# Last expert pair of a mixture-of-experts layer: other PSUM banks, later weight rows, a scatter in two halves, and one weight load issued earlier

## The chip, the cores and the metric

One Trainium2 chip, one of its cores. The metric is the device time of one execution in microseconds (us). The kernel before takes 551.63 us (median of 3 runs, 550.75 to 552.73). Engines: PE (TensorE), DVE (VectorE), ACT (ScalarE), POOL (GpSimd), and SP, which issues most of the DMAs.

## The reference

A decoder layer on 512 tokens of width 1024, float32: attention and a short convolution with their projections, a residual and a LayerNorm, then a mixture of 32 experts (each token goes to 2 of them), a residual and a second LayerNorm. The part that matters here:

```python
h2 = (x * (1.0 + scale2) + shift2).reshape(bsz * seq, d)
moe = _hierarchical_moe(h2, ...)   # per expert: silu(h @ w_gate) * (h @ w_up), weighted, @ w_down
x = _layer_norm(DEEPNORM_ALPHA * x + gate2 * moe, ln2_g[l], ln2_b[l])
```

An expert has w_gate and w_up of 1024 x 256 and w_down of 256 x 1024: three blocks of 1 MB each, 96 MB over all experts.

## The kernel before

The first 240 us compute the attention, the convolution and the modulation vectors; until about 300 us come the output projection, the first LayerNorm (x1) and the router. Every expert has 64 slots for tokens. Experts are worked on in 16 pairs (`pair(j)`, numbers 2j and 2j+1); the rows of a pair are 128 partitions, 64 for each expert.

For a pair, POOL **gathers** the rows of h2 from DRAM by an indirect DMA (L621), PE transposes them (`expert_rows`, L1612) and ACT copies them out (L833). For each expert PE then runs gate and up together (`gates`, `gate_up`, L1622, 32 instructions), ACT the silu (L846), DVE the product (`hidden`, L1247), PE a transpose of it (`turn`, L1640), ACT a copy (`hid_t`, L840), PE the down projection (`finish`, `down`, L1631) into a PSUM bank that `down_bank` names, and DVE scales its result out of that bank into the buffer ysb (`y_out`, L1256, two instructions). When both experts of a pair are out, POOL **scatters** ysb to y_dram, 2 rows for each token, by an indirect DMA (`scatter`, L627). `y_out` counts in the semaphore y_ev, and `finish(n)` waits until the bank it writes has been read: y_ev >= n if the down projection before it used the same bank.

Weights come through SP's DMA queue in a written order: `load_gu(n)` (gate and up, ring of 8 buffers, L460) and `load_dn(n)` (ring of 6, L471). A load waits for the expert that last used its buffer. The first loads wait for what else lies in their buffers: the up half of expert 7 for the last tiles of x1 (`x1_last`, which DVE writes at L1178), w_dn of expert 5 for the stores of h2 (`st_h2`, issued by ACT at L790), and the gate half of expert 8 for `gates(0)`.

The last pair, 15, is not scattered. PE builds rows of weights (`weight_rows`, L1660) from the diagonals `diag`, DVE makes from them a matrix hot_w (`last_hot`, L1280 to L1287), and PE multiplies it with ysb of that pair straight into the sum of each token tile (`last_rows`, L1737). The rest of a tile is x1 and the two rows of y_dram: SP loads x1 of tiles 0 and 1 (L532) and, when all scatters are down, eight blocks y_tok of 512 KB (L537). The residual x1 of tiles 2 and 3 was held in PSUM (tile 2 in banks 0 and 1, tile 3 in banks 4 and 5) and ACT copies it out (L892). DVE adds seven terms to x1 (`first_terms`, L1346), PE adds x1 to the sum (`other_terms`, L1744), and statistics, scaling and stores of the four tiles follow. Tiles are taken in the order 1, 2, 3, 0.

The order around the change is that of the code: each engine runs its list in order and waits on semaphores.

## Time and profile before

| | us |
|---|---|
| median of 3 runs | 551.63 |
| the profiled execution's own time | 551.87 |
| its span | 550.1 |
| PE busy | 509.8 |
| DVE busy | 285.4 |
| ACT busy | 105.5 |
| POOL busy | 101.6 |

The span is what the traced instructions cover; the execution's own time is 1.8 us longer. Busy time is the sum over the whole span. DMA traffic is given in GB/s, and as the mean busy share of the core's 16 DMA engines.

### The profile page before, as it was taken

What the parts mean: (1) busy time and instruction counts of PE and PEld (TensorE: products, weight loads), DVE (VectorE), ACT (ScalarE), POOL (GpSimd) and SP (SyncE); (2) the same over time, 40 slices, a digit from 0 to 9 for tenths busy, and PEclk for the clock granted to TensorE, in tenths of its full rate; (3) what the DMA queues carried; (4) which work ended last, traced back from release to release, by engine and by line L of the source; (5) the groups of instructions that cost most, each with busy time, mean ns of one, the idle gap of its engine ahead of it and who ended that gap; (6) DMA issues with size and microseconds to landing.
All of it is one profiled execution on the core that took longest, in us unless ns stands there. A gap on an engine that the chain in (4) does not pass through costs nothing.

```text
span 550.1 us, 6473 instructions
## 1 busy us (share of the span) xinstructions
PE 509.8 (93%) x2516; PEld 274.5 (50%) x2516; DVE 285.4 (52%) x520; ACT 105.5 (19%) x173; POOL 101.6 (18%) x111
## 2 busy tenths in 40 slices
PE   3999999999999999999996999999998799898983
PEld 2445468744444444444583555555554355444531
DVE  4664999763937393263889732232222122213388
ACT  1000211233223231200232311111111111121030
POOL 2000000061306040030452111111211011210015
PEclk9999999999999999999997999999999899989998
DMA  8999679954640244269998999999999999999763
GB/s 254 358 361 352 207 237 309 309 212 153 227 155 1 77 146 174 75 245 418 413 391 310 388 405 420 414 416 417 414 417 416 416 415 416 416 416 418 312 251 153
DMA packets 71280, 169.22 MB, mean 308 GB/s; under 512 B 7902, under 2 KB 45842, under 8 KB 63056
## 3 DMA queue, kind: packets, MB, share of 16 engines
q1 hardware_dynamic: 64304, 152.22, 73.2%
q10 hardware_dynamic: 2480, 8.44, 4.0%
q0 software_dynamic: 4464, 8.12, 3.9%
q8 instruction: 21, 0.34, 0.2%
q14 instruction: 11, 0.09, 0.0%
HBM read 159.60 MB, written 17.30 MB: 322 GB/s over the span
## 4 chain that ended last, share of the span: by engine, by line
PE 61%; DVE 14%; DMA 11%; SPq 9%; issue 3%; ACT 1%; POOL 0%; DVEq 0%; POOLq 0%; ACTq 0%
PE ps L1622 17%; PE ps L1492 11%; PE ps L1538 10%; PE ps L1631 9%; DVE acc_rows L935 5%; SPq L414 4%; DMA w_gu<-in_w_up_dram 4%; PE ps L1612 3%; PE ps L1462 3%; DMA ada_stage<-in_w_ada_dram 3%; DMA w_stage<-in_w_in_dram 2%; PE ps L1481 2%; DMA y_tok<-y_dram 2%; PE ps L1526 2%; DMA y_dram<-ysb,slot_row 1%
## 5 line engine op out<-in xcount | busy, mean ns | idle before, releaser
L1622 PE MATMUL ps<-w_gu,xT 128*64 128x256 f32 x1024 | 119.3, 386 | 3.4 <-issue 1.6
L1622 PEld LDWEIGHTS ps<-w_gu,xT 128*64 128x64 f32 x1024 | 72.0, 138 | 40.5 <-issue 3.4
L1492 PE MATMUL ps<-hT,w_stage 128*128 128x512 f32 x192 | 84.8, 595 | 0.0
L1256 DVE TENSOR_TENSOR ysb<-ps,rows_gate 64x512 f32<-64x512 f32 x64 | 44.1, 689 | 61.8 <-PE ps L1631 61.3
L1631 PE MATMUL ps<-w_dn,hidT 128*64 128x512 f32 x256 | 62.9, 612 | 7.8 <-issue 6.1
L935 DVE SCALAR_TENSOR_TENSOR acc_rows<-ada_stage,csil,acc_rows 128x256 f32<-128x256 f32 x112 | 55.2, 493 | 4.0
L1247 DVE TENSOR_TENSOR hid<-ps,silu_sb 128x128 f32<-128x128 f32 x32 | 9.3, 292 | 91.9 <-ACT silu_sb L846 91.9
L1492 PEld LDWEIGHTS ps<-hT,w_stage 128*128 128x128 f32 x192 | 35.5, 190 | 41.0 <-issue 41.0
L1538 PE MATMUL ps<-wo,mixT 128*128 128x512 f32 (+1 forms) x144 | 55.6, 545 | 0.0
L1403 PE MATMUL ps<-hT,w_first 128*128 128x512 f32 x96 | 45.5, 621 | 0.9 <-DVE hT L961 0.9
L627 POOL DMA_INDIRECT y_dram<-ysb,slot_row x15 | 15.1, 1009 | 151.8 <-DVE ysb L1256 151.8
L1538 PEld LDWEIGHTS ps<-wo,mixT 128*128 128x128 f32 x144 | 27.2, 190 | 27.1 <-issue 26.3
L1631 PEld LDWEIGHTS ps<-w_dn,hidT 128*64 128x64 f32 x256 | 17.3, 138 | 31.3 <-issue 25.9
L846 ACT ACTIVATE silu_sb<-ps 128x128 f32<-128x128 f32 x32 | 8.9, 277 | 115.9 <-PE ps L1622 115.9
L1462 PE MATMUL ps<-w_stage,hT 128*128 128x256 f32 x128 | 28.1, 380 | 0.2 <-DMA w_stage<-in_w_in_dram 0.2
L1403 PEld LDWEIGHTS ps<-hT,w_first 128*128 128x128 f32 x96 | 18.2, 199 | 20.1 <-issue 20.1
L1462 PEld LDWEIGHTS ps<-w_stage,hT 128*128 128x128 f32 x128 | 24.2, 190 | 4.3 <-DMA w_stage<-in_w_in_dram 0.6
L983 DVE TENSOR_TENSOR_SCAN stay<-stay,block_end 128x1280 f32<-128x1280 f32 x8 | 24.1, 3015 | 3.4 <-POOL stay L586 3.4
L583 POOL TENSOR_SCALAR_AFFINE_SELECT stay<-stay 128x384 f32<-128x384 f32 x8 | 5.3, 658 | 101.0 <-ACT stay L727 101.0
L947 DVE SCALAR_TENSOR_TENSOR acc_cols<-ada_in,csil,acc_cols 128x512 f32<-128x512 f32 (+1 forms) x35 | 22.6, 645 | 2.3 <-DMA ada_in<-in_w_ada_dram 1.1
L621 POOL DMA_INDIRECT xg<-h_dram,slot_tok x16 | 16.9, 1054 | 37.0 <-PE ps L1622 23.3
L1612 PEld LDWEIGHTS ps<-ident,xg 128*128 128x128 f32 x128 | 15.5, 194 | 6.6 <-issue 5.8
(213 smaller groups left out, 499.2 us busy)
## 6 DMA issues: line engine op xcount, KB each, us to landing
w_gu<-in_w_gate_dram SPq DMA_DIRECT2D x32, 1024.0 KB, 20.3
w_gu<-in_w_up_dram SPq DMA_DIRECT2D x32, 1024.0 KB, 23.3
w_dn<-in_w_down_dram SPq DMA_DIRECT2D x32, 1024.0 KB, 24.3
ada_stage<-in_w_ada_dram SPq DMA_DIRECT2D x16, 1024.0 KB, 7.8
w_stage<-in_w_in_dram SPq DMA_DIRECT2D x9, 1024.0 KB, 10.1
ada_in<-in_w_ada_dram SPq DMA_DIRECT2D x12, 512.0 KB, 9.5
y_dram<-zeros ACTq DMA_DIRECT2D x4, 1024.0 KB, 5.8
wo<-in_w_out_dram SPq DMA_DIRECT2D x2, 2048.0 KB, 13.3
```

The source lines that it names most:

```text
L414: sp.dma_start(ada_in[c][:, ks, s], rows[:, ks, s * D + k * P:s * D + (k + m) * P]).then_inc(ld_ada[c][half], 16)
L935: link(w.scalar_tensor_tensor(out=acc, in0=st[:, k], scalar=csil[:, 3, k:k + 1], in1=acc, op0=ALU.mult, op1=ALU.add))
L947: ins = w.scalar_tensor_tensor(out=acc, in0=ada_in[c][:, k], scalar=csil[:, 3, k:k + 1], in1=acc, op0=ALU.mult, op1=ALU.add)
L983: w.tensor_tensor_scan(out=st[:, 0:ZW][:, ::-1], data0=st[:, 0:ZW][:, ::-1], data1=block_end[:, ::-1], initial=1.0, op0=ALU.mult, op1=ALU. ...
L1256: ins = w.tensor_tensor(to[e * HD:(e + 1) * HD, b * 512:(b + 1) * 512], ps[b * HD:(b + 1) * HD, down_bank(y), :], gate2r[b * HD:(b + 1) * ...
L1403: ins = t.matmul(ps[:, n], w_first[:, k, n * P:(n + 1) * P], hT[:, k], start=k == 0, stop=k == KC - 1)
L1462: ins = t.matmul(dst[:, 0:CW], hT[:, k, i * P:(i + 1) * P], st[:, k], start=k == 0, stop=k == KC - 1)
L1492: ins = t.matmul(ps[:, 6], st[:, k, (f % 2) * P:(f % 2 + 1) * P], hT[:, k], start=k == 0, stop=k == KC - 1)
L1538: ins = t.matmul(ps[:, 4 + q % 4, 0:width], mixT[:, i, k], wo[n][:, k, col:col + width], start=k == 0, stop=k == KC - 1)
L1612: ins = t.transpose(flat[:, ROWS_AT + k * P:ROWS_AT + (k + 1) * P], by_channel(xg[rows_buffer(j)])[:, k], ident[:])
L1622: ins = t.matmul(ps[a * SLOTS:(a + 1) * SLOTS, GATE_BANK[e], 0:2 * P], rows_in[:, k, e * SLOTS:(e + 1) * SLOTS], weights[:, :, k, a * P:(a ...
L1631: ins = t.matmul(ps[b * SLOTS:(b + 1) * SLOTS, bank, :], hidT[e][:, a * SLOTS:(a + 1) * SLOTS], weights[:, a, b * 512:(b + 1) * 512], star ...
```

## The change

Five edits:

- **Banks.** `down_bank` gives expert 29 bank 4 and expert 31 bank 5 (before: 29 in bank 7, 31 in bank 2). For that, x1 of tiles 2 and 3 is copied out of PSUM by ACT in pair 14, behind `hid_t(28, 0)`, and no longer at the end; the copies go to a buffer of their own, `x1_sb`, in the place of the weights of expert 28. `finish(29)` waits for the copy of tile 3.
- **Weight rows.** PE builds them behind `gates(30)` and no longer ahead of it, into banks 0 and 1 (before: 3 and 6). DVE makes hot_w behind `hidden(30, 0)` and no longer ahead of it, in one multiply over 1024 columns instead of two over 512.
- **Scatter.** The rows of pair 14 go in two indirect DMAs of 64 partitions, each as soon as its expert is out. The second takes its row numbers from `late_row`, which DVE copies once.
- **Load order.** SP issues w_dn of expert 5, behind the wait for the stores of h2, ahead of the wait for `x1_last` and the up half of expert 7.
- Waits on the scatters are counted anew.

Part of the branch for overflowing experts, in which only counts change, is left out of the diff.

```diff
--- before.py
+++ after.py
@@ -153,12 +153,13 @@
         g1r = at("g1r", [P, D], REST + 48 * KB)
         b1r = at("b1r", [P, D], REST + 52 * KB)
 
-        x1_back = at("x1_back", [P, TC, D], 0)
+        x1_back = at("x1_back", [P, 2, D], 0)
         norm2 = at("norm2", [1, 2, D], 0)
         slot_id = at("slot_id", [P, TC, 2, P], EXP_B + 8 * KB)
         ones_back = at("ones_back", [P, P], EXP_B + 12 * KB)
         hot_w = at("hot_w", [P, TC, 2, P], PAIR2)
         zeros = at("zeros", [P, D], PAIR2)
+        x1_sb = at("x1_sb", [P, 2, D], PAIR2 + 4 * KB)
         y_tok = [at(f"y_tok{i}", [P, 2, D], PAIR1 + (i + 1) * 8 * KB) for i in range(TC)]
         diag = at("diag", [P, TC, 2, P], REST + 48 * KB)
         g2r = at("g2r", [P, D], PAIR1)
@@ -188,6 +189,7 @@
         wk = sm("wk", [P, 2, TC])
         mh = sm("mh", [P, 1])
         last_row = sm("last_row", [P, 1])
+        late_row = sm("late_row", [P, 1], I32)
         tile_total = sm("tile_total", [P, 2])
         colsb = sm("colsb", [P, 2 * KC])
         b_cols = sm("b_cols", [P, 2, KC])
@@ -380,7 +382,11 @@
 
         def down_bank(n):
 
-            return 2 if n == NE - 1 else 7
+            return {NE - 3: 4, NE - 1: 5}.get(n, 7)
+
+        def x1_rows_of(i):
+
+            return x1_back[:, i] if i < 2 else x1_sb[:, i - 2]
 
         def h2T_of(i):
 
@@ -496,11 +502,11 @@
             load_gu_part(GU_RING - 1, 0)
             sp.wait_ge(logit_done, TC)
             load_gu(5)
-            sp.wait_ge(x1_last, 2 + 2 * len(X1_BY_DVE))
-            load_gu_part(GU_RING - 1, 1)
             for n in range(2):
                 sp.wait_ge(st_h2[n], 32)
             load_dn(5)
+            sp.wait_ge(x1_last, 2 + 2 * len(X1_BY_DVE))
+            load_gu_part(GU_RING - 1, 1)
             load_gu(GU_RING)
             dn_next = DN_RING
             for n in range(GU_RING + 1, NE):
@@ -524,14 +530,14 @@
                                          ).then_inc(ov_ld, 16)
                         sp.dma_start(w_dn[e][:], w_down[0, bass.ds(ex, 1)].rearrange("o (a p) n -> p (o a) n", p=P)
                                      ).then_inc(ov_ld, 16)
-                sp.wait_ge(scattered[0], 16 * (NPAIR // Y_RING + NOVP))
+                sp.wait_ge(scattered[0], 16 * (NPAIR // Y_RING + 1 + NOVP))
 
 
             sp.wait_ge(n2_done, 4)
             for i in (1, 0):
                 sp.dma_start(x1_back[:, i], x1_dram.rearrange("(i p) n -> i p n", p=P)[i]).then_inc(ld_x1[i], 16)
             for n in range(Y_RING):
-                sp.wait_ge(scattered[n], 16 * ((NPAIR - n) // Y_RING))
+                sp.wait_ge(scattered[n], 16 * (NPAIR // Y_RING + 1 if n == 0 else NPAIR // Y_RING - 1))
             for i in TAIL:
                 for k in range(2):
                     sp.dma_start(y_tok[i][:, k], y_dram.rearrange("(i p k) n -> i k p n", p=P, k=2)[i, k]
@@ -539,7 +545,7 @@
             out_rows = out[0].rearrange("(i p) n -> i p n", p=P)
             for i in (2, 1, 3):
                 sp.wait_ge(fin_done[i], 1)
-                sp.dma_start(out_rows[i], x1_back[:, i]).then_inc(st_out, 16)
+                sp.dma_start(out_rows[i], x1_rows_of(i)).then_inc(st_out, 16)
             for n in range(2):
                 cols = slice(n * 512, (n + 1) * 512)
                 sp.wait_ge(fin_done[0], n + 1)
@@ -621,6 +627,13 @@
                 g.indirect_dma_start(out=buf[:], out_offset=None, in_=h2_dram,
                                      in_offset=bass.IndirectOffsetOnAxis(ap=slot_tok[:, j:j + 1], axis=0),
                                      bounds_check=T - 1, oob_is_err=False).then_inc(sem_done, 16)
+
+            def scatter_half(j, e, buf, sem_done):
+
+                rows_to = slot_row[0:SLOTS, j:j + 1] if e == 0 else late_row[0:SLOTS, 0:1]
+                g.indirect_dma_start(out=y_dram, out_offset=bass.IndirectOffsetOnAxis(ap=rows_to, axis=0),
+                                     in_=buf[e * SLOTS:(e + 1) * SLOTS], in_offset=None,
+                                     bounds_check=2 * T - 1, oob_is_err=False).then_inc(sem_done, 16)
 
             def scatter(j, buf, sem_done):
 
@@ -666,8 +679,14 @@
                     pool.wait_ge(gu_done, NE - 6)
                     g.iota(slot_id[:], [[2 * P, TC], [1, 2], [2, P]], base=0, channel_multiplier=0,
                            allow_small_or_imprecise_dtypes=True).then_inc(slot_ids, 1)
-                pool.wait_ge(y_ev, 2 * j + 2)
-                scatter(j, ysb[j % Y_RING], scattered[j % Y_RING])
+                if j == NPAIR - 2:
+                    pool.wait_ge(diag_done, 2 * TC + 2)
+                    for e in range(2):
+                        pool.wait_ge(y_ev, 2 * j + 1 + e)
+                        scatter_half(j, e, ysb[j % Y_RING], scattered[j % Y_RING])
+                else:
+                    pool.wait_ge(y_ev, 2 * j + 2)
+                    scatter(j, ysb[j % Y_RING], scattered[j % Y_RING])
 
             pool.wait_ge(flag_ready, 1)
             more = pool.value_load(flag[0:1, 0:1], min_val=0, max_val=NOVB)
@@ -862,6 +881,9 @@
                 if j == NPAIR - 3:
                     norm_rows()
                 hid_t(2 * j, 0)
+                if j == NPAIR - 2:
+                    for i in (2, 3):
+                        s.copy(x1_rows_of(i), x1_held(i)).then_inc(ld_x1[i], 16)
                 silu(2 * j + 1, 1)
                 if j + 1 < NPAIR:
                     xe_copy(j + 1)
@@ -887,9 +909,6 @@
                         act.wait_ge(tr_done, NE + 2 * j + e + 1)
                         s.copy(hidT[e][:], ps[:, GATE_BANK[e], TURN:TURN + P]).then_inc(tr_ev, 1)
 
-
-            for i in (2, 3):
-                s.copy(x1_back[:, i], x1_held(i)).then_inc(ld_x1[i], 16)
 
             act.wait_ge(summed, 2)
             s.activation(x1_back[:, 1], flat[:, 0:D], ACT.Identity, accum_out=tile_total[:, 0:1]).then_inc(totals, 1)
@@ -1261,8 +1280,9 @@
             def pair(j):
                 if j == NPAIR - 1:
                     y_out(2 * j - 1, 1)
+                hidden(2 * j, 0)
+                if j == NPAIR - 1:
                     last_hot()
-                hidden(2 * j, 0)
                 if 0 < j < NPAIR - 1:
                     y_out(2 * j - 1, 1)
                 if j == 0:
@@ -1278,12 +1298,9 @@
                 dve.wait_ge(slot_ids, 1)
                 dve.wait_ge(w_rows, 1)
                 link(w.tensor_copy(last_row[:], slot_row[:, NPAIR - 1:NPAIR]))
-                for b in range(2):
-                    some = slice(b * TC // 2, (b + 1) * TC // 2)
-                    did(w.scalar_tensor_tensor(out=hot_w[:, some].rearrange("p c k t -> p (c k t)"),
-                                               in0=slot_id[:, some].rearrange("p c k t -> p (c k t)"), scalar=last_row[:, 0:1],
-                                               in1=ps[:, (3, GATE_BANK[1])[b]], op0=ALU.is_equal, op1=ALU.mult))
-                settle()
+                link(w.scalar_tensor_tensor(out=hot_w.rearrange("p c k t -> p (c k t)"),
+                                            in0=slot_id.rearrange("p c k t -> p (c k t)"), scalar=last_row[:, 0:1],
+                                            in1=flat[:, 0:2 * T], op0=ALU.is_equal, op1=ALU.mult))
                 w.tensor_tensor(hot_w[:, :, 0], hot_w[:, :, 0], hot_w[:, :, 1], ALU.add).then_inc(hot_ready, 1)
 
             dve.wait_ge(row_ev, 8)
@@ -1296,6 +1313,7 @@
             for i in range(TC):
                 for k in range(2):
                     w.tensor_scalar(diag[:, i, k], ident[:], wk[:, k, i:i + 1], None, ALU.mult).then_inc(diag_done, 1)
+            w.tensor_copy(late_row[0:SLOTS], slot_row[SLOTS:2 * SLOTS, NPAIR - 2:NPAIR - 1]).then_inc(diag_done, 1)
             pair(NPAIR - 2)
             pair(NPAIR - 1)
             y_out(NE - 1, 1)
...
@@ -1324,13 +1342,13 @@
             def centre(i, src):
 
                 settle()
-                w.scalar_tensor_tensor(out=x1_back[:, i], in0=src, scalar=mv[:, TC + i, 0:1], in1=g2r[:],
+                w.scalar_tensor_tensor(out=x1_rows_of(i), in0=src, scalar=mv[:, TC + i, 0:1], in1=g2r[:],
                                        op0=ALU.subtract, op1=ALU.mult).then_inc(centred, 1)
 
             def finish(i, cols):
 
                 dve.wait_ge(rstd_done, norm_at(TC + i) + 1)
-                w.scalar_tensor_tensor(out=x1_back[:, i, cols], in0=x1_back[:, i, cols], scalar=rstd[:, TC + i:TC + i + 1],
+                w.scalar_tensor_tensor(out=x1_rows_of(i)[:, cols], in0=x1_rows_of(i)[:, cols], scalar=rstd[:, TC + i:TC + i + 1],
                                        in1=bb2r[:, cols], op0=ALU.mult, op1=ALU.add).then_inc(fin_done[i], 1)
 
             def tile_sum(i):
@@ -1343,8 +1361,8 @@
                 dve.wait_ge(ld_x1[i], 16)
                 for k in range(n):
                     dve.wait_ge(ld_y[i][k], 16)
-                    ins = w.scalar_tensor_tensor(out=x1_back[:, i], in0=y_tok[i][:, k], scalar=wk[:, k, i:i + 1],
-                                                 in1=x1_back[:, i], op0=ALU.mult, op1=ALU.add)
+                    ins = w.scalar_tensor_tensor(out=x1_rows_of(i), in0=y_tok[i][:, k], scalar=wk[:, k, i:i + 1],
+                                                 in1=x1_rows_of(i), op0=ALU.mult, op1=ALU.add)
                     if k + 1 < n:
                         link(ins)
                 ins.then_inc(partial, 1)
@@ -1650,14 +1668,17 @@
                 pe.wait_ge(ld_dn[n % DN_RING], 16 * (n // DN_RING + 1))
                 if n >= 1:
                     pe.wait_ge(y_ev, n if down_bank(n) == down_bank(n - 1) else n - 1)
+                if n == NE - 3:
+                    pe.wait_ge(ld_x1[3], 16)
                 down(n % 2, w_dn[n % DN_RING], dn_done, down_bank(n))
 
             def weight_rows():
 
                 pe.wait_ge(diag_done, 2 * TC + 1)
+                pe.wait_ge(ld_x1[2], 16)
                 for i in range(TC):
                     for k in range(2):
-                        ins = t.matmul(ps[:, (3, GATE_BANK[1])[i // 2], (2 * (i % 2) + k) * P:(2 * (i % 2) + k + 1) * P], ones_back[:], diag[:, i, k], start=True, stop=True)
+                        ins = t.matmul(flat[:, (2 * i + k) * P:(2 * i + k + 1) * P], ones_back[:], diag[:, i, k], start=True, stop=True)
                 ins.then_inc(w_rows, 1)
 
             def norm_rows():
@@ -1675,9 +1696,10 @@
                     turn(2 * j - 1, 1)
                     if j == NPAIR - 1:
                         finish(2 * j - 1)
-                        weight_rows()
                     pe.wait_ge(xe_ev, j + 1)
                     gates(2 * j)
+                    if j == NPAIR - 1:
+                        weight_rows()
                     if j < NPAIR - 1:
                         finish(2 * j - 1)
                     if j == NPAIR - 3:
@@ -1741,7 +1763,7 @@
 
                 pe.wait_ge(partial, TAIL.index(i) + 1)
                 for n in range(2):
-                    ins = t.matmul(ps[:, sum_bank(i) + n], ident[:], x1_back[:, i, n * 512:(n + 1) * 512],
+                    ins = t.matmul(ps[:, sum_bank(i) + n], ident[:], x1_rows_of(i)[:, n * 512:(n + 1) * 512],
                                    start=False, stop=not by_pe)
                     if not by_pe:
                         ins.then_inc(summed, 1)
@@ -1752,11 +1774,9 @@
                                  start=False, stop=True).then_inc(summed, 1)
 
             pe.wait_ge(y_ev, NE)
-            pe.wait_ge(ld_x1[2], 16)
             last_rows(1)
             last_rows(2)
             other_terms(1, False)
-            pe.wait_ge(ld_x1[3], 16)
             last_rows(3)
             other_terms(2, False)
             last_rows(0)
```

**PE**, the last pair: `down` of expert 28, `turn` and `down` of expert 29, and the weight rows between the down projection and the gate and up of expert 30 (L1660). Before:

```order
L1631 MATMUL ps<-w_dn_61,hidT_164 64x512 x4
L1640 MATMUL ps<-ident,hid_141 128x128
L1631 MATMUL ps<-w_dn_62,hidT_165 64x512 x4
L1660 MATMUL ps<-diag,ones_back 128x128 x8
L1622 MATMUL ps<-w_gu_55,xT_117 64x256 x16
L1640 MATMUL ps<-ident,hid_140 128x128
L1622 MATMUL ps<-w_gu_56,xT_117 64x256 x16
```

The same place in the changed kernel, whose line numbers are its own:

```order
L1649 MATMUL ps<-w_dn_61,hidT_166 64x512 x4
L1658 MATMUL ps<-ident,hid_142 128x128
L1649 MATMUL ps<-w_dn_62,hidT_167 64x512 x4
L1640 MATMUL ps<-w_gu_55,xT_117 64x256 x16
L1681 MATMUL ps<-diag,ones_back 128x128 x8
L1658 MATMUL ps<-ident,hid_141 128x128
L1640 MATMUL ps<-w_gu_56,xT_117 64x256 x16
```

The eight matmuls of the weight rows moved from ahead of the gate and up of expert 30 to behind it; what PE does is otherwise in the same order.

**SP**, the first loads that wait, about 283 to 307 us; w_gu_54 and w_dn_62 belong to expert 5, w_gu_56 to expert 7, w_gu_49 to expert 8, and the waits stand in brackets. Before:

```order
L460 DMA w_gu_54<-in_w_up_dram 128x2048
L460 DMA w_gu_56<-in_w_up_dram 128x2048 [waits x1_last]
L471 DMA w_dn_62<-in_w_down_dram 128x2x1024 [waits st_h21,st_h20]
L460 DMA w_gu_49<-in_w_gate_dram 128x2048 [waits gu_done]
L460 DMA w_gu_49<-in_w_up_dram 128x2048
```

In the changed kernel:

```order
L466 DMA w_gu_54<-in_w_up_dram 128x2048
L477 DMA w_dn_62<-in_w_down_dram 128x2x1024 [waits st_h21,st_h20]
L466 DMA w_gu_56<-in_w_up_dram 128x2048 [waits x1_last]
L466 DMA w_gu_49<-in_w_gate_dram 128x2048 [waits gu_done]
L466 DMA w_gu_49<-in_w_up_dram 128x2048
```

Two rows changed places: w_dn of expert 5 now waits for its own two semaphores alone.

## Rows read from the trace of the kernel before

**Rows 1.** The page, the span in 40 equal slices: DMA share in tenths, and GB/s.

```profile
DMA  8999679954640244269998999999999999999763
GB/s 254 358 361 352 207 237 309 309 212 153 227 155 1 77 146 174 75 245 418 413 391 310 388 405 420 414 416 417 414 417 416 416 415 416 416 416 418 312 251 153
```

**Rows 2.** The chain that ended last: start us, us, what.

```profile
476.45 22.89 DMA w_gu<-in_w_up_dram
...
511.75 6.79 DMA y_dram<-ysb,slot_row
...
519.39 9.22 DMA y_tok<-y_dram
```

**Rows 3.** Timeline 503 to 517 us: start, us, engine line op, operands, [idle before <-releaser].

```profile
503.11 0.28 ACT L846 ACTIVATE silu_sb<-ps 128x128 f32<-128x128 f32 x1 [3.76 <-PE ps L1622]
506.32 0.27 ACT L840 COPY hidT<-ps 128x128 f32<-128x128 f32 x1 [1.12 <-PE ps L1640]
507.60 1.94 PE L1631 MATMUL ps<-w_dn,hidT 128*64 128x512 f32 x8 [1.32 <-DVE ysb L1256]
509.47 2.05 PE L1660 MATMUL ps<-diag,ones_back 128*128 128x128 f32 x16
509.58 1.39 DVE L1256 TENSOR_TENSOR ysb<-ps,rows_gate 64x512 f32<-64x512 f32 x2 [2.12 <-PE ps L1631]
511.45 3.67 PE L1622 MATMUL ps<-w_gu,xT 128*64 128x256 f32 x32
515.83 0.33 PE L1640 MATMUL ps<-ident,hid 128*128 128x128 f32 x1 [0.70 <-DVE hid L1247]
516.09 3.67 PE L1622 MATMUL ps<-w_gu,xT 128*64 128x256 f32 x32
```

**Rows 4.** Loads of w_gu: the up half of expert 31, issued at 490.1 us.

```profile
DMA to landing us min/median/max: 25.4/25.4/25.4
```

**Rows 5.** Loads of x1 for tiles 1 and 0, issued at 500.1 and 501.6 us.

```profile
DMA to landing us min/median/max: 22.0/22.2/22.3
```

**Rows 6.** The eight loads of y_tok, issued from 518.55 to 522.0 us.

```profile
DMA to landing us min/median/max: 6.3/10.4/12.9
```

**Rows 7.** Timeline 522 to 529 us, the end of the last pair.

```profile
522.73 1.93 ACT L892 COPY x_back<-ps 128x1024 f32<-128x1024 f32 x2 [0.69 <-issue]
524.08 1.39 DVE L1256 TENSOR_TENSOR ysb<-ps,rows_gate 64x512 f32<-64x512 f32 x2 [1.16 <-PE ps L1631]
527.13 1.28 DVE L1346 SCALAR_TENSOR_TENSOR x_back<-y_tok,wk,x_back 128x1024 f32<-128x1024 f32 x1 [0.35 <-DMA y_tok<-y_dram]
528.71 6.32 DVE L1346 SCALAR_TENSOR_TENSOR x_back<-y_tok,wk,x_back 128x1024 f32<-128x1024 f32 x5 [0.29 <-DMA y_tok<-y_dram]
```

**Rows 8.** Windows: us, busy (x) of PE, PEld, DVE, ACT, POOL, PEclk, DMA share, GB/s.

```profile
299.00:300.00 1.00, 1.00 (x3) 0.47 (x2) 1.00 (x2) 0.00 (x0) 0.90 (x2) 0.50 0.12 49
301.00:302.00 1.00, 1.00 (x3) 0.19 (x1) 0.93 (x4) 0.00 (x0) 0.78 (x1) 1.00 0.17 54
306.00:309.00 3.00, 2.20 (x19) 1.20 (x17) 1.63 (x10) 0.54 (x2) 0.00 (x0) 1.00 1.03 403
518.00:519.00 1.00, 1.00 (x14) 0.64 (x12) 0.00 (x0) 0.00 (x0) 0.00 (x0) 1.00 0.27 111
```

**Rows 9.** SP's timeline: w_dn of expert 5, gate half of expert 8.

```profile
302.09 0.38 SPq L471 DMA_DIRECT2D w_dn<-in_w_down_dram  x1
307.30 0.33 SPq L460 DMA_DIRECT2D w_gu<-in_w_gate_dram  x1
```

**Rows 10.** Landing of w_gu of expert 8, issued at 307.3 and 307.7 us.

```profile
DMA to landing us min/median/max: 5.6/6.6/7.7
```

**Rows 11.** Landing of gathers 0 and 1, issued at 298.0 and 301.2 us; PE's timeline.

```profile
DMA to landing us min/median/max: 4.1/4.1/4.1
...
DMA to landing us min/median/max: 7.7/7.7/7.7
...
302.15 1.16 PE L1612 MATMUL ps<-ident,xg 128*128 128x128 f32 x8
```

More of the change, by code:

```diff
@@ L1305, in _ @@
                 with dve.Fori(0, NOVP) as j:
-                    dve.wait_ge(scattered[0], 16 * (NPAIR // Y_RING) + 16 * j)
+                    dve.wait_ge(scattered[0], 16 * (NPAIR // Y_RING + 1) + 16 * j)
                     for e in range(2):
```

## The prediction

> **What bounds the kernel now.** I first read the page's 40 slices [rows 1]. From about 310 us to 508 us the core moves 388 to 420 GB/s in nearly every slice, with the share of DMA time at nine tenths or more: the stream of expert weights runs without a gap. Only the last three slices fall off. Then the chain that ended last [rows 2]: at its end stand a weight load (up half of expert 29, issued 476.45, down at 499.34), the last scatter (6.79 us) and the loads of y_tok (9.22 us). So the last 50 us are a race between the DMA queues and PE, and I took the timeline there and asked for each load when it landed.
>
> PE in that stretch [rows 3]: `finish(29)` starts at 507.60, having waited 1.32 us for `y_out(28)` because both use bank 7; weight rows 509.47; `gates(30)` 511.45; a wait of 0.70 for the product; `gates(31)` 516.09. The up half of expert 31 was issued at 490.1 and took 25.4 us [rows 4]: it is down at 515.5, only 0.6 us before PE uses it.
>
> The views that decide are those of landings. The x1 tiles were issued at 500.1 and 501.6 and need 22.3 and 22.0 us [rows 5]: 522.4 and 523.6. The eight y_tok loads, issued from 518.55, land first after 6.3 us (524.85) and last after 12.9 (522.0 + 12.9 = 534.9) [rows 6]. Eight tiles between 523.6 and 534.9 are 1.3 to 1.4 us for each, which is what 512 KB take at 400 GB/s. So the first y_tok comes one tile's time behind the last x1 tile, although it was issued 5 us before that tile was down. In the same time the window 518 to 519 shows a DMA share of 0.27 and 111 GB/s [rows 8]: about 4 of 16 engines still work on what was queued, the others are empty. A load is down when the slowest engine has done its part. The y_tok tiles are therefore held by a few engines that are late, not by their issue.
>
> DVE ends the last pair at 524.08 + 1.39 = 525.5 and goes through seven terms; it waits 0.35 and 0.29 us for y_tok and then runs on without a wait, one term in 1.3 us, as fast as the late engines deliver [rows 7]. What follows (statistics, scaling, stores) hangs on these terms.
>
> **The change part by part.**
>
> *Bank of expert 29.* `finish(29)` then needs only its transposed input, whose copy ends at 506.32 + 0.27 = 506.59 [rows 3]. It starts at about 506.65: 0.95 us earlier. Its new wait, for ACT's copy of tile 3, costs nothing: both copies take 1.93 us [rows 7] and are put into a gap of ACT of 3.76 us that ends at 503.11 [rows 3], so they are done at about 501.3. Behind `finish(29)` on PE is `gates(30)`.
>
> *Weight rows.* Without them ahead of it (509.47 to 511.45, 1.98 us) `gates(30)` could start 0.95 + 1.98 = 2.9 us earlier, at 508.5. Its weights are the question. The trace gives no landing for the up half of expert 30. The bounds are 499.34 (expert 29's, [rows 2]) and 511.45, when PE used it without a wait [rows 3]. Six blocks of 1 MB come down between 499.34 and 515.5, 2.7 us each; two of them behind this one, so 515.5 - 5.4 = 510.1. I take 510.1. Then 3.67 for `gates(30)`, 1.98 for the weight rows, which cover the wait of 0.70, and 0.3 for `turn(30)`: `gates(31)` at 516.05, against 516.09. The 2.9 us won by the two edits are spent on a weight load that is not there yet (1.6) and on the weight rows that now stand between two pieces of work (1.3). Ends: with the weights at 508.5 or before, `gates(31)` is held by its own load at 515.5, a gain of 0.6; with 511.45 it starts at 517.4, a loss of 1.3. `last_hot` on DVE has until 525.5 and costs nothing there (DVE is idle for most of this time); the second half of hot_w in one instruction instead of two changes nothing either.
>
> *Bank of expert 31 and the copies at the end.* ACT's two copies end at 524.66 [rows 7], before `y_out(31)` at 525.5, which PE waits for as well. Taking them away gives nothing.
>
> *Scatter in halves.* `y_out(29)`, at 509.58 [rows 3], comes 0.95 us earlier, and with it the second half: issued at 510.8 instead of 511.75 [rows 2]. The first half is issued some 3 us before. Landing of the second: not later than a whole one, 510.8 + 6.8 = 517.6; not earlier than its packets in a quiet queue, the 4.1 us of the first gather [rows 11], 514.9. I take 516.5, so y_tok is issued 2 us earlier, and the quick engines finish earlier. The late ones have x1 tiles in front until 523.6 whatever the issue time, so the term is 0. Its ends: 0 and, if the issue did count, what DVE can take: its waits (0.64) and what PE gains (0.6), 1.2 us.
>
> The Trainium skill, "DMA: Bandwidth & Descriptors", section "Anatomy of one DMA", fits a DMA issued by POOL as 2.0 us plus its bytes at 436 GB/s. By that a half scatter of 256 KB would need 2.6 us as an estimate, where the whole one shows 6.79 [rows 2]; the sum would stay what it is, since the x1 tiles stand in front all the same.
>
> *w_dn of expert 5 earlier.* It was issued at 302.09 [rows 9]; the new place lets it go when the stores of h2 are down, some 6 us earlier. There the DMA is nearly idle (shares 0.12 and 0.17 [rows 8]), and 1 MB is 2.5 us at 416 GB/s. But the hole is moved, not filled. The next load, expert 8, waits for `gates(0)` and is issued at 307.30 [rows 9]. In the kernel before, w_dn and two gathers keep the engines full until then (306 to 309: share 1.03 [rows 8]), and expert 8 lands at 307.7 + 7.7 = 315.4 [rows 10], so its 2 MB (5.0 us) began at about 310. Afterwards they can begin at 307.3 plus 0.8 us from issue to movement (as y_tok: 518.55 to 519.39), 308.1, plus 0.6 for a gather that still shares the queue: 308.7. Against that, the first gather, which PE takes at once at 302.15 [rows 11], now shares the engines with w_dn. Its delay is between 0 and 3.6 us (a gather behind a load took 7.7 us, this one 4.1 [rows 11]). I take 0.8, because w_dn ends at about 301.5 and the gather's own bytes are 0.6 us. `gates(0)` and the load of expert 8 come 0.8 later: 309.5 instead of 310. From there the stream has no gap [rows 1], so its end moves as its beginning: **0.5 us earlier**, between 1.3 earlier and 2.3 later.
>
> Sum: 0 + 0 + 0 + 0 - 0.5, from the profiled execution's own 551.87, gives 551.4. That execution is 0.24 us above the median of 551.63, so on the scale of the medians 551.1 to 551.4; I say **551.3**. Less than 0.3% (1.65 us, about what a measurement of this kernel can tell from no change).
>
> **The rivals.**
>
> *Faster: issue and PE do count.* If the late engines catch up, or are others in the changed kernel, the tail is held by DVE and by `gates(31)`: 0.6 to its load, 0.64 of waits, and 0.5 to 1.0 of the earlier stream, 1.7 to 2.3 us: 549.7. For it: y_tok moves 2 us earlier, and the chain runs through it [rows 2]. Against it: landings of x1 and y_tok follow each other without a hole [rows 5, 6].
>
> *Slower: the first gather is held up.* If gather 0, with a load queued in front and one beside it, takes the 7.7 us of gather 1 [rows 11], PE starts 3.6 us later and expert 8's load with it: 308.1 + 3.6 = 311.7, and the gather beside it is then through; 1.7 to 2.3 us later than now. The stream ends that much later, and so does everything behind it: 553.8. It decides from a delay of 1.3 us on, where the 0.5 us of gain is gone. Against it: the engines run dry in that stretch, so w_dn can be in the way for its own 2.5 us only.
>
> The same page of the Trainium skill, section "Queues, rings and completion order", says that an engine takes turns between its queues, packet by packet. By that the gather is delayed by about its own length, an estimate nearer to my 0.8 than to 3.6.
>
> *Same time, other reason: weight rows in the way.* If expert 30's weights land at 511.45 only, the tail is up to 1.3 us later, less the 0.5: 552.4, still within the bound unless it comes together with the gather.
>
> **How the numbers follow.** Forecast 0.60, weight rows in the way 0.08 (also "no change"), issue counts 0.21, gather held up 0.08, small ends of both 0.03. So faster by over 0.3%: 0.22; within: 0.67; slower: 0.11. The likeliest is the forecast, 551.3. The range goes down to 549.3, a little below the faster rival, and up to 552.9, which takes in the weight rows but not all of the gather.
>
> **What would show it.** In the changed profile: `down` of expert 29 with no wait for DVE, at about 506.6; a wait of `gates(30)` for DMA of 1 to 2 us; weight rows ahead of `turn(30)`, and `gates(31)` within 0.6 us of 516; y_tok issued near 516.9, but the first of them landing 8 us later instead of 6.3; the DVE terms still waiting for y_tok. Early on: w_dn of expert 5 issued near 296.4, the first gather landing in about 5 us, and a DMA share clearly under 1 between 306 and 308. I am wrong if y_tok lands as much earlier as it is issued, if `gates(30)` finds its weights at 508.5, or if the first gather is late by more than 1.3 us.

## The result, and the profile after

The changed kernel takes 553.36 us (median of 21 runs, 551.59 to 555.68), the kernel before in the same comparison 551.67 (21 runs, 550.00 to 552.73): a ratio of 1.0034, with a 95% interval of 1.0023 to 1.0045. It is slower by 1.7 us (difference of the medians). I had forecast 551.3 and no change, with a range up to 552.9; the slower side had 0.11.

The profiled execution took 552.76 us (span 551.0). Its page, the lines that answer to [rows 1]:

```profile
DMA  9999679854640264179999899999999999999863
GB/s 272 356 362 350 220 240 314 295 187 152 230 153 1 77 197 150 48 295 419 413 391 364 306 385 420 414 415 419 415 415 416 415 416 417 416 416 417 307 237 152
```

The stream of weights is as full as before from slice 24 on (385 to 420 GB/s). The difference in the middle is in slices 22 and 23, about 289 to 316 us: 364 and 306 GB/s instead of 310 and 388, that is more traffic ahead of the experts and less at their start.

The executions compared here differ by up to 1.7 us in what comes ahead of the experts, so absolute times of two profiles can't be subtracted. I count from a landmark that no edit touches, PE's first bf16 matmul of the router, the first line below for each kernel. PE's timeline, before and changed, from the landmark to the first gate and up:

```profile
293.57 0.23 PE L1590 MATMUL ps<-mb,before 128*128 128x128 bf16 x1 [2.51 <-DVE mb L1110]
...
303.59 3.67 PE L1622 MATMUL ps<-w_gu,xT 128*64 128x256 f32 x32 [0.28 <-ACT xT L871]
```

```profile
292.36 0.23 PE L1608 MATMUL ps<-mb,before 128*128 128x128 bf16 x1 [2.51 <-DVE mb L1129]
...
302.66 1.16 PE L1630 MATMUL ps<-ident,xg 128*128 128x128 f32 x8 [1.62 <-DMA xg<-h_dram,slot_tok]
304.11 3.67 PE L1640 MATMUL ps<-w_gu,xT 128*64 128x256 f32 x32 [0.28 <-ACT xT L893]
```

`gates(0)` started 10.02 us behind the landmark and now starts 11.75 behind it: **1.73 us later**, which is the size of the loss. PE now idles 1.62 us for the gathered rows, which it had not done. Why, is in SP's and POOL's timeline and in two landings (changed kernel; the last two lines are the landing of w_dn and that of the gather):

```profile
294.67 0.38 SPq L477 DMA_DIRECT2D w_dn<-in_w_down_dram  x1
...
296.79 1.40 POOL L627 DMA_INDIRECT xg<-h_dram,slot_tok  x1 [10.65 <-DVE slot_tok L1167]
...
307.82 0.33 SPq L466 DMA_DIRECT2D w_gu<-in_w_gate_dram  x1
...
DMA to landing us min/median/max: 7.3/7.3/7.3
...
DMA to landing us min/median/max: 5.8/5.8/5.8
```

w_dn of expert 5 goes out 2.1 us ahead of the gather. It is down only after 7.3 us, at 301.97, and the gather 0.6 us behind it, at 302.59: after 5.8 us instead of 4.1 [rows 11]. Expert 8's load is issued 15.46 us behind the landmark; it had been 307.30 - 293.57 = 13.73. The windows of the changed kernel at the same place (columns as in [rows 8]):

```profile
300.00:301.00 1.00, 1.00 (x3) 0.19 (x1) 0.90 (x5) 0.00 (x0) 1.00 (x1) 1.00 0.70 271
301.00:302.00 1.00, 0.04 (x1) 0.00 (x0) 0.86 (x5) 0.00 (x0) 0.29 (x1) 1.00 0.57 98
306.00:309.00 3.00, 2.20 (x21) 1.19 (x19) 0.69 (x4) 0.33 (x2) 0.00 (x0) 1.00 0.47 104
```

The hole has moved, from 299 to 302 (0.12 and 0.17 in [rows 8]) to 306 to 309, where the share falls from 1.03 to 0.47, and PE got a hole of its own beside it. (Counted from the landmark, the window of the changed kernel is 307.21 to 310.21 in the kernel before; the share there is 1.06.) What this does to the weight stream is in two windows, the first 40 us behind the landmark and the 175 us after that: before, changed, and the kernel of the filler experiment below, in which PE alone starts late.

```profile
293.57:333.57 40.00, 37.15 (x263) 20.31 (x265) 23.27 (x68) 7.87 (x18) 7.64 (x7) 0.91 0.94 373
333.57:508.57 175.00, 164.42 (x1143) 87.66 (x1141) 44.50 (x86) 29.07 (x68) 26.35 (x26) 0.98 1.02 416
```

```profile
292.36:332.36 40.00, 35.53 (x256) 19.88 (x258) 22.55 (x67) 7.73 (x17) 7.66 (x7) 0.91 0.91 356
332.36:507.36 175.00, 166.38 (x1144) 88.66 (x1140) 44.12 (x87) 30.82 (x69) 26.34 (x26) 0.97 1.02 416
```

```profile
292.66:332.66 40.00, 37.15 (x260) 20.73 (x262) 22.73 (x67) 7.73 (x17) 7.64 (x7) 0.91 0.92 360
332.66:507.66 175.00, 164.47 (x1144) 87.46 (x1140) 44.94 (x87) 29.26 (x68) 26.34 (x26) 0.98 1.02 416
```

In the first 40 us the changed kernel moves 17 GB/s less, 0.68 MB in all, which is 1.6 us of the stream at 416 GB/s. From then on all three move the same 416 GB/s at a share of 1.02, so nothing of it is made good.

The end of the last pair, PE's and POOL's timeline of the changed kernel, which answers to [rows 3]:

```profile
507.37 0.27 ACT L859 COPY hidT<-ps 128x128 f32<-128x128 f32 x1 [1.11 <-PE ps L1658]
507.69 1.94 PE L1649 MATMUL ps<-w_dn,hidT 128*64 128x512 f32 x8 [0.35 <-ACT hidT L859]
509.34 0.93 POOL L634 DMA_INDIRECT y_dram<-ysb,slot_row  x1 [5.84 <-DVE ysb L1275]
510.92 3.67 PE L1640 MATMUL ps<-w_gu,xT 128*64 128x256 f32 x32 [1.30 <-issue]
511.84 0.90 POOL L634 DMA_INDIRECT y_dram<-ysb,late_row  x1 [1.57 <-DVE ysb L1275]
514.52 2.05 PE L1681 MATMUL ps<-diag,ones_back 128*128 128x128 f32 x16
516.41 0.27 PE L1658 MATMUL ps<-ident,hid 128*128 128x128 f32 x1
```

`finish(29)` follows its input's copy and no longer waits for DVE. `gates(30)` stands still for 1.30 us ("issue": nothing in the profile releases it). That it waits for its weights is inferred: their load has no landing in this trace, and the other waits in front of this instruction are for work that was long done. The weight rows follow it. The landings of y_tok and DVE's waits for them, which answer to [rows 6, 7]:

```profile
L543 SPq DMA_DIRECT2D y_tok<-y_dram x8: 319/588/1255, 517.8 to 522.9; - x8
DMA to landing us min/median/max: 7.3/11.3/12.9
```

```profile
528.38 1.28 DVE L1364 SCALAR_TENSOR_TENSOR x_back<-y_tok,wk,x_back 128x1024 f32<-128x1024 f32 x1 [1.06 <-DMA y_tok<-y_dram]
```

The first tile lands at 517.8 + 7.3 = 525.1. Behind the landmark it is issued at 225.4 and lands at 232.7, where it had been 225.0 and 231.3: what the halves win here is less than what the late start costs.

### The profile page after: what moved, and what is told of

The parts are those of the page before. It is cut to its first block, busy times and chain, and to the rows that moved or that the text cites. A ratio compares the mean times of both kernels' runs of the same rounds, so it can differ in the third digit from the quotient of the medians.

```text
span 551.0 us, 6477 instructions
## 1 busy us (share of the span) xinstructions
PE 511.1 (93%) x2516; PEld 275.7 (50%) x2516; DVE 285.3 (52%) x520; ACT 105.5 (19%) x173; POOL 102.7 (19%) x112
## 4 chain that ended last, share of the span: by engine, by line
PE 74%; DVE 10%; DMA 9%; issue 2%; SPq 2%; ACT 1%; POOL 0%; DVEq 0%; ACTq 0%; POOLq 0%
PE ps L1640 17%; PE ps L1510 11%; PE ps L1556 10%; PE ps L1649 8%; PE ps L1421 8%; PE ps L1480 5%; DMA w_gu<-in_w_up_dram 5%; PE ps L1630 3%; PE ps L1473 2%; DMA y_tok<-y_dram 2%; PE ps L1499 2%; SPq L466 1%; DVE acc_rows L954 1%; DVE stay L1002 1%; PE ps L1544 1%
## 5 line engine op out<-in xcount | busy, mean ns | idle before, releaser
L1640 PE MATMUL ps<-w_gu,xT 128*64 128x256 f32 x1024 | 121.9, 392 | 4.3 <-DMA w_gu<-in_w_up_dram 2.4
L1640 PEld LDWEIGHTS ps<-w_gu,xT 128*64 128x64 f32 x1024 | 73.5, 141 | 43.2 <-issue 6.3
L1649 PE MATMUL ps<-w_dn,hidT 128*64 128x512 f32 x256 | 61.4, 599 | 6.6 <-issue 5.8
L1630 PE MATMUL ps<-ident,xg 128*128 128x128 f32 x128 | 18.5, 288 | 1.6 <-DMA xg<-h_dram,slot_tok 1.6
```

The source lines that it names most:

```text
L1630: ins = t.transpose(flat[:, ROWS_AT + k * P:ROWS_AT + (k + 1) * P], by_channel(xg[rows_buffer(j)])[:, k], ident[:])
L1640: ins = t.matmul(ps[a * SLOTS:(a + 1) * SLOTS, GATE_BANK[e], 0:2 * P], rows_in[:, k, e * SLOTS:(e + 1) * SLOTS], weights[:, :, k, a * P:(a ...
L1649: ins = t.matmul(ps[b * SLOTS:(b + 1) * SLOTS, bank, :], hidT[e][:, a * SLOTS:(a + 1) * SLOTS], weights[:, a, b * 512:(b + 1) * 512], star ...
```

## The experiments

Theory G: the first gather shares the DMA engines with w_dn of expert 5, PE starts the experts late, and the lateness stays to the end. Rivals: W, the weight rows are in the way in the last pair; S, the split scatter disturbs the tail. All ratios are to the kernel before in the same comparison, with their 95% intervals; a loss in us is the ratio times 551 us unless it is called a difference of medians. The first four kernels below were compared with the same 29 runs of the kernel before, so their ratios share that sample's error.

### The load order alone, and without it

`e1_order_only` is the kernel before with one edit; `e2_undo_order` is the changed kernel with that edit taken back.

```diff
+            for n in range(2):
+                sp.wait_ge(st_h2[n], 32)
+            load_dn(5)
             sp.wait_ge(x1_last, 2 + 2 * len(X1_BY_DVE))
             load_gu_part(GU_RING - 1, 1)
-            for n in range(2):
-                sp.wait_ge(st_h2[n], 32)
-            load_dn(5)
```

> The kernel before with nothing changed but the place of w_dn of expert 5 in SP's order. Theory G (the first gather shares the DMA engines with w_dn, PE starts the experts late, expert 8's load and the whole stream behind it start late): gather 0 lands in 5.5 to 6.2 us instead of 4.1, gates(0) starts about 1.7 us later against the router's end, and the median is 1.3 to 2.0 us above that of before, nearly the whole loss of 1.7 us. Theory W (weight rows in the way at the end of the last pair): no difference to before, below 0.4 us. Theory S (the split scatter disturbs the tail): no difference either.

> The changed kernel with w_dn of expert 5 back at its old place; banks, weight rows and the scatter in halves as changed. Theory G: gather 0 lands in about 4.1 us again and the median is that of before within 0.5 us. Theory W or S: still 1 to 2 us above before.

Measured: the order alone 1.0052 (1.0039 to 1.0064), 2.9 us, more than the 1.3 to 2.0 that G had said (the medians differ by 2.3); the change without it 1.0014 (1.0002 to 1.0025), 0.8 us (0.4 by the medians), where the change with it had 1.0034. The timeline of the order alone:

```profile
295.18 0.38 SPq L471 DMA_DIRECT2D w_dn<-in_w_down_dram  x1
...
303.17 1.16 PE L1612 MATMUL ps<-ident,xg 128*128 128x128 f32 x8 [2.34 <-DMA xg<-h_dram,slot_tok]
304.62 3.67 PE L1622 MATMUL ps<-w_gu,xT 128*64 128x256 f32 x32 [0.29 <-ACT xT L871]
```

Its landmark is at 292.88, so `gates(0)` starts 11.74 behind it, 1.72 late; the gather landed in 5.8 us, and in 4.4 us with the edit undone. One window of the order alone shows how the engines finish:

```profile
301.00:302.00 1.00, 0.00 (x0) 0.00 (x0) 0.79 (x8) 0.00 (x0) 0.88 (x1) 1.00 0.43 135
```

w_dn again takes 7.3 us and is down at 302.5. From 301 to 302 the share is down to 0.43, so most of the work is through, but PE stands still (0.00) until the gather is down at 303.2. That the gather waits for a few late engines is my reading of this share; the trace doesn't show each engine. G holds, W and S can't be the main loss.

### The other two parts, each alone

`e3_halves_only` is the kernel before with the scatter of pair 14 in halves (the diff shows the main part; the copy into `late_row` and the counts go with it); `e4_banks_rows_only` has the banks, the earlier copies and the later weight rows, and neither the halves nor the load order.

```diff
-                pool.wait_ge(y_ev, 2 * j + 2)
-                scatter(j, ysb[j % Y_RING], scattered[j % Y_RING])
+                if j == NPAIR - 2:
+                    for e in range(2):
+                        pool.wait_ge(y_ev, 2 * j + 1 + e)
+                        scatter_half(j, e, ysb[j % Y_RING], scattered[j % Y_RING])
```

> The kernel before with the scatter of pair 14 in halves and nothing else. Slow-engine theory: y_tok is issued 0.5 to 1 us earlier (y_out(29) is where it was, only the second half is shorter), but the landings of y_tok and the time stay: within 0.4 us of before. Rival (the issue of y_tok counts): 0.3 to 1 us faster. Theory S: slower by 0.5 us or more.

> The changed kernel with the old load order and the whole scatter: only the banks, the earlier copies of x1 and the later weight rows are left. My prediction's sum: gates(30) waits for its weights, gates(31) starts within 0.6 us of where it was, time within 0.4 us of before. Theory W: gates(31) starts 0.5 to 1.3 us later against the weight stream and the median is up to 1 us above before. Theory G: no difference.

Measured: halves 1.0012 (1.0000 to 1.0024), banks and rows 1.0013 (1.0001 to 1.0025): about 0.7 us each by the ratio (0.3 and 0.8 by the medians), with intervals that begin at no change, and no gain in either. Both are above the 0.4 us that I had allowed. The profile of the halves alone:

```profile
516.24 1.66 SPq L538 DMA_DIRECT2D y_tok<-y_dram  x2
```

```profile
DMA to landing us min/median/max: 7.5/11.1/12.7
```

From its landmark (292.77) y_tok is issued at 223.47, where before it was at 518.55 - 293.57 = 224.98: 1.5 us earlier. The first tile lands at 231.0 against 231.3, and the last of the seven terms ends at 241.5 in both profiles. The issue is 1.5 us earlier and the landing 0.3, so the issue is not what holds the tiles. That they wait for engines that are late, as I had argued, fits this but isn't shown. In the profile of banks and rows, the chain that ended last shows where the time won on PE goes:

```profile
506.77 1.94 PE ps L1642 x8
508.71 2.10 issue
510.81 3.67 PE ps L1633 x32
514.49 1.98 PE ps L1674 x16
```

`gates(30)` could start at 508.71 and stands still for 2.10 us; then the weight rows take 1.98. `gates(31)` starts 222.93 behind the landmark (293.58) against 222.52: 0.4 us later.

More of this shows with the kernels of the next sections. Against the kernel that lacks only banks, weight rows and halves, `gates(31)` comes 0.64 us later in the changed kernel, 0.51 with half of w_dn early, 0.92 with w_dn behind the gather, and 0.01 earlier with the old order; the last instruction comes 0.95, 0.48 and 0.87 later and 0.10 earlier. So in three of four pairs the edits at the tail make the end later. In each of them PE goes from `gates(30)` through the weight rows to `gates(31)` without a stop, 5.7 us from start to start, so the rows stand in the way; but the last load of w_gu is down later as well, by 0.65, 0.96, 0.89 and 0.41 us. These profiles don't part the two, and why the load is later was not found.

### A late start of PE by itself

To part PE's late start from what w_dn does to the DMA stream, `e5_late_pe` leaves the load order as it was and adds two filler matmuls ahead of the first gathered rows; `e12_later_pe` adds four.

```diff
-            for n in range(3):
+            for n in range(5):
                 t.matmul(ps[:, ROW_BANK[6]], ones[:], gate2r[:, 0:512], start=True, stop=True)
```

> The kernel before with two more filler matmuls ahead of the first gathered rows, whose result nobody reads: gates(0) starts about 1.7 us later, as with the new load order, but w_dn of expert 5 stays where it was and keeps the DMA engines busy meanwhile. Theory G2 (the loss is the idle hole of the DMA stream ahead of expert 8's load, not PE's late start): expert 8's load is issued 1.7 us later but queues behind w_dn all the same, so the stream loses only about 0.5 us and the time rises by 0.3 to 0.9 us. Theory P (PE's late start is the loss by itself, passed on to the end one to one): 1.7 us or more above before.

Measured: 1.0039 (1.0024 to 1.0055), 2.2 us (1.8 by the medians). I had argued for G2, 0.3 to 0.9 us; the interval leaves that out, and P (the late start is the loss by itself) holds.

```profile
292.66 0.23 PE L1590 MATMUL ps<-mb,before 128*128 128x128 bf16 x1 [2.51 <-DVE mb L1110]
...
304.25 1.08 PE L1622 MATMUL ps<-w_gu,xT 128*64 128x256 f32 x8 [0.28 <-ACT xT L871]
```

`gates(0)` is 11.59 behind the landmark, 1.57 late, with the gather as quick as before (4.0 us). So a loss of this size comes from PE's late start alone, without w_dn in an earlier place. The windows above show how: expert 8's load waits for `gates(0)`, and the stream is 13 GB/s x 40 us = 0.52 MB behind, or 1.25 us at 416 GB/s. The load order alone is behind by the same (360 GB/s). In this profile the last instruction comes 1.0 us later than before, though, less than the runs lose.

> The kernel before with four more filler matmuls ahead of the first gathered rows instead of two; their result is read by nobody. gates(0) starts about 3.3 us later than in before, twice the delay of the run with two. Theory P: the time follows, 3 to 4.2 us above before (1.0055 to 1.0076). Rival (the loss with two fillers was a step, such as another place of DMA traffic, and not a delay passed on): about the same 2 us as with two.

Measured: 1.0063 (1.0040 to 1.0085), 3.5 us (3.2 by the medians), for a start that is 305.20 - 292.05 - 10.02 = 3.13 us late. By the runs, lateness is passed on about one to one, over 245 us, and it is no step. By the profiles the last instruction comes 1.0 us later with two fillers and 2.5 with four: one to one from the first to the second, and about 0.6 us less than the lateness in both.

### How much of the load, and when

`e6_half_early` sends half of w_dn of expert 5 early and half at the old place, in the kernel before; `e7_change_half_early` does it in the changed kernel. (The definition of `load_dn_half`, a DMA of 512 KB, and the count that `finish` waits for are left out.)

```diff
+            for n in range(2):
+                sp.wait_ge(st_h2[n], 32)
+            load_dn_half(5, 0)
             sp.wait_ge(x1_last, 2 + 2 * len(X1_BY_DVE))
             load_gu_part(GU_RING - 1, 1)
-            for n in range(2):
-                sp.wait_ge(st_h2[n], 32)
-            load_dn(5)
+            load_dn_half(5, 1)
```

> The kernel before with w_dn of expert 5 loaded in two DMAs: the first half (512 KB) at the new early place, the second behind the up half of expert 7, at the old one. Theory G: the first half is through before the first gather's packets are ready (300.5 in the profile with the whole block early), so gather 0 lands in about 4.1 us and gates(0) is not late; the second half and the gathers keep the engines busy until expert 8's load comes; the stream is up to 1.2 us earlier and the time 0.5 to 1.3 us below before. Rival (any load at the early place delays the gather, whatever its size): gather 0 in 5 us or more and a time 1 us or more above before.

> The changed kernel with its banks, weight rows and scatter in halves, and w_dn of expert 5 half early and half at the old place. Theory G: as the half-early kernel against before, so 0 to 1 us below before and 2 us or more below the changed kernel. Rival: as the changed kernel.

Measured: 1.0009 (0.9994 to 1.0023) and 1.0021 (1.0004 to 1.0038). The gain that I expected did not come in either, and the second is 0.7 us below the changed kernel, not 2. The gather took 4.6 and 4.8 us even with half the block ahead of it, and `gates(0)` was 0.5 us late in the first (302.45 with the landmark at 291.90) and 0.7 in the second.

`e9_behind_gather` (diff) and `e10_beside_gather` (the same with + 0 for + 1) keep w_dn whole and hold it until later, at 2.6 and 1.4 us behind the gather's issue; `e11_change_behind_gather` is the first of them in the changed kernel.

```diff
+            for n in range(2):
+                sp.wait_ge(st_h2[n], 32)
+            sp.wait_ge(x1_last, 2 + len(X1_BY_DVE) + 1)
+            load_dn(5)
             sp.wait_ge(x1_last, 2 + 2 * len(X1_BY_DVE))
             load_gu_part(GU_RING - 1, 1)
-            for n in range(2):
-                sp.wait_ge(st_h2[n], 32)
-            load_dn(5)
```

> The kernel before with w_dn of expert 5 ahead of the up half of expert 7, but held until the first of the last two x1 instructions of DVE is done (about 300.5 on before's clock, 2.5 us behind the issue of gather 0): its packets come right behind those of gather 0 and fill the hole up to the up half of expert 7. Theory P (what counts is when gates(0) starts): gather 0 lands in 4.1 to 4.4 us, gates(0) is where it was, and the time is that of before or up to 1 us below, since the hole ahead of expert 8's load grows no larger than what is saved. Rival H (the loss is w_dn leaving its old place behind the up half of expert 7, where it kept the engines busy until expert 8's load): 1 us or more above before.

> The same, held only until about 299.4, when both multiplications of DVE are done: w_dn starts to move at about 300.4, in the middle of gather 0's packets. Theory P: gather 0 lands 0.3 to 1 us later than in before, gates(0) with it, and the time is 0 to 1.2 us above before, between the kernel that holds it longer and the one that does not hold it. Rival H: as the one held longer, 1 us or more above.

> The changed kernel, with w_dn of expert 5 held until about 300.5 as above. Theory P: the loss of the change goes, within 0.8 us of before and 1 us or more below the changed kernel. Rival H: as the changed kernel.

Measured: 1.0005 (0.9988 to 1.0022), 1.0010 (0.9986 to 1.0033), and 1.0017 (0.9997 to 1.0036) in the changed kernel. The gather landed after 4.3, 4.2 and 4.2 us; for the second I had expected 0.3 us or more of delay. The window of the first of them, at the place where w_dn used to be:

```profile
306.00:309.00 3.00, 2.20 (x19) 1.20 (x17) 1.81 (x11) 0.54 (x2) 0.00 (x0) 1.00 0.95 302
```

Here w_dn stands in the order in which the change has it, the gather is quick (4.3 us), and in the kernel before the loss is gone. So the order as such is not the loss. Rival H is answered in part only: held back like this, w_dn keeps the engines busy until expert 8's load all the same (share 0.95), so this run doesn't tell what an empty stretch there costs by itself. That the stream was filled earlier gained nothing that can be measured either.

In the changed kernel the test is not clear. By the ratio the loss halves, from 1.0034 to 1.0017, with intervals that overlap; by the medians it is 1.6 us against 1.7, and the last instruction of the profile comes 1.2 us late with `gates(0)` only 0.17 late. I had said 1 us or more below the changed kernel. What is left there goes with the banks, rows and halves (1.0014 without the order, 0.4 us by the medians), and is not explained in full.

`e8_change_again` was a second profile of the changed kernel.

> The changed kernel once more, for a second profile. Theory G: gather 0 lands 1.4 to 2.5 us later than the 4.1 of before, gates(0) with it, and the end of the weight stream, counted from the router's first bf16 matmul, is 1.3 to 2.0 us later than before.

Its gather landed after 5.5 us and made PE wait 1.54, and `gates(0)` began 303.40 - 291.96 = 11.44 behind the landmark, 1.42 late. The up half of expert 31 is down 2.0 us later than before (490.26 + 25.7 - 291.96 = 224.0 against 222.0), the upper end of what I had said.

All kernels by the start of `gates(0)`. The second and third columns are from one profiled execution each, counted from the landmark; the last two are from all runs.

| kernel | `gates(0)` later than before, us | last instruction later, us | medians differ by, us | ratio (95% interval) |
|---|---|---|---|---|
| banks and rows | 0.13 | 0.3 | 0.8 | 1.0013 (1.0001 to 1.0025) |
| w_dn held 1.4 us behind the gather | 0.13 | -0.2 | 0.5 | 1.0010 (0.9986 to 1.0033) |
| the change, w_dn held 2.6 us behind the gather | 0.17 | 1.2 | 1.6 | 1.0017 (0.9997 to 1.0036) |
| w_dn held 2.6 us behind the gather | 0.21 | 0.3 | 0.6 | 1.0005 (0.9988 to 1.0022) |
| the change, old load order | 0.25 | -0.1 | 0.4 | 1.0014 (1.0002 to 1.0025) |
| halves | 0.34 | 0.1 | 0.3 | 1.0012 (1.0000 to 1.0024) |
| half of w_dn early | 0.53 | 0.5 | 0.4 | 1.0009 (0.9994 to 1.0023) |
| the change, half of w_dn early | 0.74 | 1.0 | 0.7 | 1.0021 (1.0004 to 1.0038) |
| two fillers more | 1.57 | 1.0 | 1.8 | 1.0039 (1.0024 to 1.0055) |
| load order alone | 1.72 | 1.2 | 2.3 | 1.0052 (1.0039 to 1.0064) |
| the change | 1.73 | 2.1 | 1.7 | 1.0034 (1.0023 to 1.0045) |
| the change, second profile | 1.42 | 2.3 | | |
| four fillers more | 3.13 | 2.5 | 3.2 | 1.0063 (1.0040 to 1.0085) |

Differences of 0.3 us in the first column stand between kernels whose early part is the same (halves, banks and rows), so no less than that can be read from it. None of the variants beats the kernel before.

## Why the prediction was wrong

**The step that failed is "w_dn of expert 5 earlier", in two places.** First its delay of the gather: I gave bounds of 0 and 3.6 us and took 0.8, because w_dn would be through at 301.5 and the gather's own bytes are 0.6 us. It was 1.7. That the gather follows w_dn by its own length held: the gather was down 0.6 us behind w_dn. The end of w_dn did not: 301.5 is 7.9 us behind the landmark, and w_dn was down 9.6 behind it, although it was issued a little earlier than I had said. I had reckoned with 2.5 us for 1 MB in a DMA that is nearly idle; from issue to landing it took 7.3, and what counts is when the last part of it is down, the argument that I had used for y_tok myself.

Second, what a delay costs: I let the beginning of the stream absorb part of it (0.5 us of gain left over, "decides from 1.3 us on"). The gain was not there. With the load order alone the stream moved 0.52 MB less in the first 40 us, 1.25 us, and no run that filled the hole without delaying the gather was faster than before. Whether an allowance of about 0.5 us is left is open: the medians and ratios of the filler runs show none (1.57 us late cost 1.8 or 2.2, 3.13 cost 3.2 or 3.5), their profiles show about 0.6.

The rival "the first gather is held up" had the mechanism and the place, with 0.08; its price (1.7 to 2.3 us) was right and its delay (3.6 us) too large for it. With 1.7 for the delay and one to one for its price the sum would have been 553.3 against the measured 553.36. So near a match is partly luck: in the profiles the order alone makes the end 1.2 us later, and banks, rows and halves 0.9 more.

The Trainium skill ("DMA: Bandwidth & Descriptors", section "Queues, rings and completion order") has an engine take turns between its queues, from which I had estimated a delay of about the gather's own length. The measured delay of 1.7 us is nearly three times that length of 0.6 us.

**Right:** the bank of expert 29 (`finish(29)` at once behind its input, 0.35 us of wait instead of 1.32). `gates(30)` stands still for 1.25 to 1.30 or 2.09 to 2.10 us in the six profiles with the later weight rows (1.6 forecast). The halves landed after 5.6 and 5.9 us (5.7 forecast for the second). With the old order y_tok is issued 2.0 us earlier, as forecast, and its first tile lands after 8.1 us instead of 6.3, 0.2 us earlier.

**Half right:** the weight rows. `gates(31)` was to be within 0.6 us of its old start. It is 0.4 us late with banks and rows alone, and 0.5 to 0.9 in three of four pairs of kernels that differ by the tail edits: the rival "weight rows in the way" may have a share in the loss. Its own term can't be told from the later landing of expert 31's weights (0.4 to 1.0 us in the same pairs), for which the sum had no term. Whether the 0.7 us that the ratios show for the halves alone are real is open; that profile shows nothing of it.

**Open too:** profiles and runs don't agree kernel by kernel. The order alone ends its last instruction 255.6 us behind the landmark, before 254.4: 1.2 us, against 2.9 in the ratio and 2.3 in the medians; the whole change ends 2.1 and 2.3 us later, against 1.9 and 1.7. The profiled run of the order alone (552.34) is the quickest of its kernel's five, so part of it is spread between executions; the rest was not found.

## What to carry to other kernels

A hole in the DMA traffic ahead of a small, urgent transfer is not free space: a block put there delayed that transfer, and what counted was when the block was down, not how long its bytes are. Before filling such a hole, look at who waits for the next transfer. If that engine's start releases the refills of a stream that later runs without a gap, price the delay at nearly its full length: a full DMA share later on means that nothing is made good.

## What the runs showed of the hardware that I had not expected

The first gather, 4.0 to 4.5 us from issue to landing, took 4.6 and 4.8 us with 512 KB issued 2.4 and 1.8 us ahead of it, and 5.5 to 5.8 us with 1 MB issued 2.1 to 2.6 us ahead of it. Yet in the kernel before, the engines stand idle for 2.8 of the 4 us from 298.57 to 302.57 (share 0.31), and 1 MB is 2.5 us at 416 GB/s. The same 1 MB issued 1.4 us behind the gather left it at 4.2 us. And a start 1.6 us late was still there 245 us later (1.8 us by the medians, 1.0 in the profile), through a stretch in which the DMA share stood at 1.02.
